# The order of the k-tiles inside a unit of matmuls, and the start of two moving operands

## The chip, the cores and the metric
The kernel runs on one core of one Trainium2 chip. The metric is the device time of one execution in microseconds (us).

## The reference
One decoder layer over 256 prompt tokens with 16 learned meta tokens ahead of them, and 8 sample tokens. It computes, with RMS norms ahead of both halves and at the end:

```python
h = rmsnorm(x, norm1_g)
z = h @ w_in                       # u, cg, bg, q, k, v, o, gates, g_a, g_b
conv_out, sc = causal_dwconv(cg * u, sc0, w_shortconv)
a_out = bg * conv_out
hb, (c, n, m) = mlstm_sequence(qh, kh, vh, ig, lf, state0, first)
mix = sigmoid(g_a) * a_out + sigmoid(g_b) * (sigmoid(o) * hb)
x = x + mix @ w_out
up, fc = causal_dwconv(rmsnorm(x, norm2_g) @ w_up, fc0, w_ffconv)
x = x + (silu(up[..., D_FF:]) * up[..., :D_FF]) @ w_down
```
D_MODEL is 2048, D_FF is 5632, there are 8 heads, all values are fp32. The outputs are the final norm of x and the new states.

## The kernel before
Features lie on the partitions and tokens in the columns. A product with fp32 accuracy is made from three products in the type fp32r: each operand is split into a high part and the rest, and hi x hi, hi weights x low data and low weights x hi data are summed in one PSUM bank.

All large products go through one routine. A **unit** (`unit`, line 1517) is 8 k-tiles of 128 rows of a weight matrix (6 in the last unit of a down strip), times 128 output columns. It makes three runs over its k-tiles: w_hi x data_hi (line 1526), w_hi x data_lo (line 1530), w_lo x data_hi (line 1534); each step is one weight load of 128 x 128 and one matmul. A **strip** (`strip`, line 1539) is two units, that is 16 k-tiles (three units and 22 k-tiles in `down_strip`, line 1666), accumulated in one bank. Four banks and four weight slots go round.

The order of the strips is written out. For each of 8 heads, `front` and `back` on the tensor engine run 16 strips on xh/xl (`mix_strip`, line 1556): strip 0 makes the head's queries (268 columns, starting at column C0 = 12), strip 1 the keys and strips 2 and 3 the values (280 columns); strips 4 to 9 make u, C, B and the three gates of the first 128 features of the head, strips 10 to 15 those of the other 128 (268 columns). After strip 4 come small matmuls and transposes for the scores (line 1587 and `turn`, line 1405), after strip 10 those for the head's values and state. Then 16 strips of the output projection on mh/ml (`out_strip`, `out_unit`, 266 columns), then twice (c = 0, 1) 44 strips of the up-projection on x2h/x2l (`up_strip`, 266 columns) and 16 strips of the down-projection on hh/hl (`down_strip`, 264 columns).

One row of k-tile data on a partition takes 280 x 4 = 1120 bytes in xh and xl, MW x 4 = 272 x 4 = 1088 bytes in x2h, x2l, mh and ml, and 264 x 4 = 1056 bytes in hh and hl. A weight k-tile takes 512 bytes. The layout puts xh at byte 34,432 of a partition (a multiple of 64), x2h at 34,464 (xh's place and 32 bytes), mh at 134,432 and the weight slots at multiples of 512 and 128 bytes. With MX = 4 (line 48) the data of x2 and of mix start 16 bytes into their rows.

Other engines: SP loads the raw weights of a unit once its slot is free; ScalarE makes w_hi (line 713) after the unit that used the slot has ended (`unit_used`); VectorE makes w_lo (line 984), takes finished banks out of PSUM (`evacuated`), writes mh/ml (lines 1245, 1248), x2h/x2l (lines 1280, 1283) and hh/hl (lines 1339, 1341), and GpSimd takes part in the gates and in the product of the feed-forward part. `unit` waits once for w_hi and once for w_lo; in its first run it takes waits tied to a k-tile: `evacuated` at k-tile 2 of a strip's last unit (so that the next strip's bank is free), and `tiles_ready` where the data are fresh.

## Time and profile before

| | us |
|---|---|
| median of 2 runs | 1700.74 (1700.73 to 1700.75) |
| the profiled execution | 1700.78 |
| its span | 1699.0 |
| PE matmul busy / weight load busy | 1688.1 / 1682.0 |
| VectorE, ScalarE, GpSimd busy | 1194.5, 766.9, 479.8 |
| chain that ended last: PE | 99% |

PE's matmuls overlap each other in the records (one lasts some 285 ns while the next starts 122 ns later), so its pace is read from the starts: a row of the view in order of time gives the start of a run of eight, and eight matmuls later the next row's start. The granted clock is 1.00 in all stretches but the first microseconds and the end. The DMA engines are busy 78% of the time in the first half and 62% in the second.

### The profile page before, as it was taken

What the parts mean: (1) busy time and instruction counts of PE and PEld (TensorE: products, weight loads), DVE (VectorE), ACT (ScalarE), POOL (GpSimd) and SP (SyncE); (2) the same over time, 40 slices, a digit from 0 to 9 for tenths busy, and PEclk for the clock granted to TensorE, in tenths of its full rate; (3) what the DMA queues carried; (4) which work ended last, traced back from release to release, by engine and by line L of the source; (5) the groups of instructions that cost most, each with busy time, mean ns of one, the idle gap of its engine ahead of it and who ended that gap; (6) DMA issues with size and microseconds to landing.
All of it is one profiled execution on the core that took longest, in us unless ns stands there. A gap on an engine that the chain in (4) does not pass through costs nothing.

```text
span 1699.0 us, 37193 instructions
## 1 busy us (share of the span) xinstructions
PE 1688.1 (99%) x13726; PEld 1682.0 (99%) x13726; DVE 1194.5 (70%) x1901; ACT 766.9 (45%) x916; POOL 479.8 (28%) x501
## 2 busy tenths in 40 slices
PE   9999999999999999999999999999999999999997
PEld 8999999999999999999999999999999999999997
DVE  5875857677585767758688877877455777777554
ACT  6545435353443535344444554544333434334443
POOL 4432414242241524224333222221000222222220
PEclk9999999999999999999999999999999999999999
DMA  8788786878778687787766666656666666666663
GB/s 204 192 222 199 197 212 168 216 177 219 192 190 216 166 216 179 212 194 195 193 177 186 189 175 184 185 173 176 183 181 182 182 179 179 179 179 178 183 176 120
DMA packets 591165, 318.80 MB, mean 188 GB/s; under 512 B 17684, under 2 KB 585988, under 8 KB 588988
## 3 DMA queue, kind: packets, MB, share of 16 engines
q1 hardware_dynamic: 578564, 292.99, 63.8%
q10 hardware_dynamic: 10448, 21.57, 5.0%
q0 software_dynamic: 2064, 2.92, 0.8%
q8 instruction: 72, 1.18, 0.3%
q14 instruction: 17, 0.14, 0.0%
HBM read 305.09 MB, written 12.78 MB: 187 GB/s over the span
## 4 chain that ended last, share of the span: by engine, by line
PE 99%; ACT 0%; POOL 0%; DVE 0%; issue 0%; ACTq 0%; POOLq 0%; DVEq 0%
PE strip L1526 32%; PE strip L1530 32%; PE strip L1534 32%; PE aux L1405 1%; PE aux L1413 1%; PE strip L1457 0%; PE aux L1587 0%; PE aux L1477 0%; PE strip L1470 0%; PE aux L1617 0%; PE aux L1616 0%; PE aux L1630 0%; PE strip L1405 0%; PE aux L1621 0%; PE aux L1622 0%; PE aux L1614 0%
## 5 line engine op out<-in xcount | busy, mean ns | idle before, releaser
L713 ACT ACTIVATE w_hi<-w_raw 128x1024 fp32r<-128x1024 f32 x557 | 588.6, 1060 | 787.7 <-PE strip L1534 755.9
L984 DVE TENSOR_TENSOR w_lo<-w_raw,w_hi 128x1024 fp32r<-128x1024 f32 x556 | 708.7, 1278 | 296.5 <-ACT w_hi L713 295.8
L1526 PE MATMUL strip<-xh,w_hi 128*128 128x268 f32 (+1 forms) x2016 | 290.9, 286 | 0.0
L1530 PE MATMUL strip<-xl,w_hi 128*128 128x268 f32 (+1 forms) x2016 | 290.0, 286 | 0.0
L1534 PE MATMUL strip<-xh,w_lo 128*128 128x268 f32 (+1 forms) x2016 | 290.0, 286 | 0.0
L1526 PEld LDWEIGHTS strip<-xh,w_hi 128*128 128x128 f32 x2016 | 265.1, 188 | 0.2
L1534 PEld LDWEIGHTS strip<-xh,w_lo 128*128 128x128 f32 x2016 | 265.2, 188 | 0.0
L1530 PEld LDWEIGHTS strip<-xl,w_hi 128*128 128x128 f32 x2016 | 265.2, 188 | 0.0
L1526 PE MATMUL strip<-x2h,w_hi 128*128 128x266 f32 x1408 | 200.1, 284 | 0.0
L1530 PE MATMUL strip<-x2l,w_hi 128*128 128x266 f32 x1408 | 199.9, 284 | 0.0
L1534 PE MATMUL strip<-x2h,w_lo 128*128 128x266 f32 x1408 | 199.9, 284 | 0.0
L1526 PEld LDWEIGHTS strip<-x2h,w_hi 128*128 128x128 f32 x1408 | 183.2, 189 | 0.1
L1534 PEld LDWEIGHTS strip<-x2h,w_lo 128*128 128x128 f32 x1408 | 183.2, 189 | 0.0
L1530 PEld LDWEIGHTS strip<-x2l,w_hi 128*128 128x128 f32 x1408 | 183.1, 189 | 0.0
L684 POOL TENSOR_TENSOR gg<-sg,cz 128x264 f32<-128x264 f32 x44 | 57.9, 1317 | 409.2 <-ACT sg L929 409.2
L687 POOL TENSOR_TENSOR hid<-gg,cz 128x264 f32<-128x264 f32 x44 | 73.6, 1674 | 101.7 <-DVE cz L1333 101.7
L1526 PE MATMUL strip<-hh,w_hi 128*128 128x264 f32 x704 | 102.2, 286 | 0.0
L1534 PE MATMUL strip<-hh,w_lo 128*128 128x264 f32 x704 | 101.3, 285 | 0.0
L1530 PE MATMUL strip<-hl,w_hi 128*128 128x264 f32 x704 | 101.2, 284 | 0.0
L1534 PEld LDWEIGHTS strip<-hh,w_lo 128*128 128x128 f32 x704 | 92.2, 189 | 0.0
L1530 PEld LDWEIGHTS strip<-hl,w_hi 128*128 128x128 f32 x704 | 91.9, 188 | 0.0
L1526 PEld LDWEIGHTS strip<-hh,w_hi 128*128 128x128 f32 x704 | 91.7, 188 | 0.0
(330 smaller groups left out, 1534.4 us busy)
## 6 DMA issues: line engine op xcount, KB each, us to landing
w_raw<-in_w_in SPq DMA_DIRECT2D x256, 512.0 KB, 4.5
w_raw<-in_w_up SPq DMA_DIRECT2D x176, 512.0 KB, 4.1
w_raw<-in_w_down SPq DMA_DIRECT2D x64, 512.0 KB, 4.0
w_raw<-in_w_out SPq DMA_DIRECT2D x32, 512.0 KB, 4.5
w_raw<-in_w_down SPq DMA_DIRECT2D x32, 384.0 KB, 3.4
out<-c_st ACTq DMA_DIRECT2D x8, 1024.0 KB, 7.0
c_st<-in_state_mlstm_C ACTq DMA_DIRECT2D x7, 1024.0 KB, 10.4
rb<-scratch_rows ACTq DMA_DIRECT2D x8, 270.0 KB, 5.3
```

The source lines that it names most:

```text
L684: g.tensor_tensor(gg[:, :], sg[:, :], cz[:, 0, :], ALU.mult).then_inc(gg_done, 1)
L687: g.tensor_tensor(hid[:, :], gg[:, :], cz[:, 1, :], ALU.mult).then_inc(hid_done, 1)
L713: act.activation(w_hi[:, slot, :], w_raw[:, slot, :], ACT.Copy).then_inc(hi_done, 1)
L984: v.tensor_tensor(w_lo[:, slot, :], w_raw[:, slot, :], w_hi[:, slot, :].bitcast(f32), ALU.subtract).then_inc(lo_done, 1)
L1405: return pe.transpose(out, in_, ident[0:k, 0:k])
L1413: pe.matmul(aux[1][:, 0:NM], ones[:, :], acc[:, :], start=True, stop=True)
L1526: pe.matmul(bank[b][:, 0:c1 - c0], w_hi[:, slot, w], rh[:, k0 + k, c0:c1], start=(first and k == 0), stop=False)
L1530: pe.matmul(bank[b][:, 0:c1 - c0], w_hi[:, slot, w], rl[:, k0 + k, c0:c1], start=False, stop=False)
L1534: mm = pe.matmul(bank[b][:, 0:c1 - c0], w_lo[:, slot, w], rh[:, k0 + k, c0:c1], start=False, stop=(last and k == kk - 1))
```

## The change
The change gives `unit` an argument `order`. It is the order in which each of the three runs goes through the unit's k-tiles. `range` is the order of before. `by_threes` takes 0, 3, 6, 1, 4, 7, 2, 5 (0, 3, 1, 4, 2, 5 in a unit of six). `backwards` takes 7 down to 0. The strips 1 to 9 of each head go by threes, strips 0 and 10 to 15 backwards, the up-projection of c = 1 backwards, the down-projection of c = 0 by threes; the output projection, the up-projection of c = 0 and the down-projection of c = 1 keep their order. In head 0 strips 0 and 1 are made by another routine and are not touched. The waits tied to a k-tile stay tied to that k-tile, wherever it comes. And x2h and x2l start 32 bytes earlier, the data of mh and ml start at column 0 (MM) of their rows in place of 4.

```diff
--- before.py
+++ after.py
@@ -45,7 +45,7 @@
     NM = NT - M0
     PM = TP - M0
     NF = NT - NMETA
-    MX = 4
+    MX, MM = 4, 0
     MW = (MX + NM + 7) // 8 * 8
     T2 = TP - 2 * P
     TL = NT - 2 * P
@@ -114,8 +114,8 @@
         sb("x_parts", [P, 2 * KT * NT])
         xh = nc.alloc_sbuf_tensor_at("xh", [P, KT, NT], f32r, offset=x_parts)
         xl = nc.alloc_sbuf_tensor_at("xl", [P, KT, NT], f32r, offset=x_parts + KT * NT * 4)
-        x2h = nc.alloc_sbuf_tensor_at("x2h", [P, KT, MW], f32r, offset=x_parts + 32)
-        x2l = nc.alloc_sbuf_tensor_at("x2l", [P, KT, MW], f32r, offset=x_parts + 32 + KT * NT * 4)
+        x2h = nc.alloc_sbuf_tensor_at("x2h", [P, KT, MW], f32r, offset=x_parts)
+        x2l = nc.alloc_sbuf_tensor_at("x2l", [P, KT, MW], f32r, offset=x_parts + KT * NT * 4)
         w_raw = sb("w_raw", [P, RING, KU * P])
         w_hi = sb("w_hi", [P, RING, KU * P], f32r)
         w_lo = sb("w_lo", [P, RING, KU * P], f32r)
@@ -1242,11 +1242,11 @@
                                             1.0, None, ALU.mult).then_inc(conv_step, 1)
                         if (k == 26 and jj == 0) or (k == 19 and jj == 1):
                             v.wait_ge(mixed, j + 1)
-                            v.tensor_scalar(mh[:, bass.ds(j, 1), MX:MX + NM].rearrange("p a t -> p (a t)"), mx[:, :], 1.0, None,
+                            v.tensor_scalar(mh[:, bass.ds(j, 1), MM:MM + NM].rearrange("p a t -> p (a t)"), mx[:, :], 1.0, None,
                                             ALU.mult).then_inc(mix_split, 1)
                             v.wait_ge(mix_split, j * 2 + 1)
-                            v.tensor_tensor(ml[:, bass.ds(j, 1), MX:MX + NM].rearrange("p a t -> p (a t)"), mx[:, :],
-                                            mh[:, bass.ds(j, 1), MX:MX + NM].rearrange("p a t -> p (a t)").bitcast(f32),
+                            v.tensor_tensor(ml[:, bass.ds(j, 1), MM:MM + NM].rearrange("p a t -> p (a t)"), mx[:, :],
+                                            mh[:, bass.ds(j, 1), MM:MM + NM].rearrange("p a t -> p (a t)").bitcast(f32),
                                             ALU.subtract).then_inc(mix_split, 1)
 
             front(0, first=True)
@@ -1514,29 +1514,36 @@
                 turn(aux[2][:, t * P:(t + 1) * P], sc_rows[:, t, :], P)
             turn(aux[2][:, 2 * P:2 * P + NS * H], n_rows[:, :], NS * H).then_inc(f_turned, 1)
 
-            def unit(u, slot, b, k0, kk, rh, rl, c0, c1, first, last, waits=(), frees=1):
-
-
+            def by_threes(kk):
+                return list(range(0, kk, 3)) + list(range(1, kk, 3)) + list(range(2, kk, 3))
+
+            def backwards(kk):
+                return list(range(kk - 1, -1, -1))
+
+            def unit(u, slot, b, k0, kk, rh, rl, c0, c1, first, last, waits=(), frees=1, order=range):
+
+
+                ks = order(kk)
                 pe.wait_ge(hi_done, u + 1)
-                for k in range(kk):
+                for k in ks:
                     for at_k, sm, value in waits:
                         if at_k == k:
                             pe.wait_ge(sm, value)
                     w = slice(k * P, (k + 1) * P)
                     pe.matmul(bank[b][:, 0:c1 - c0], w_hi[:, slot, w], rh[:, k0 + k, c0:c1],
-                              start=(first and k == 0), stop=False)
-                for k in range(kk):
+                              start=(first and k == ks[0]), stop=False)
+                for k in ks:
                     w = slice(k * P, (k + 1) * P)
                     pe.matmul(bank[b][:, 0:c1 - c0], w_hi[:, slot, w], rl[:, k0 + k, c0:c1], start=False, stop=False)
                 pe.wait_ge(lo_done, u + 1 + RING)
-                for k in range(kk):
+                for k in ks:
                     w = slice(k * P, (k + 1) * P)
                     mm = pe.matmul(bank[b][:, 0:c1 - c0], w_lo[:, slot, w], rh[:, k0 + k, c0:c1],
-                                   start=False, stop=(last and k == kk - 1))
+                                   start=False, stop=(last and k == ks[-1]))
                 if frees:
                     mm.then_inc(unit_used, frees)
 
-            def strip(s, u, i, b, rh, rl, c0, c1, need=(), between=None):
+            def strip(s, u, i, b, rh, rl, c0, c1, need=(), between=None, order=range):
 
 
 
@@ -1546,7 +1553,8 @@
                     waits = [(k - h * KU, sm, x) for k, sm, x in need if k // KU == h]
                     if h == 1:
                         waits.append((2, evacuated, s + 2))
-                    unit(u + h, (i + h) % RING, b, h * KU, KU, rh, rl, c0, c1, h == 0, h == 1, waits)
+                    unit(u + h, (i + h) % RING, b, h * KU, KU, rh, rl, c0, c1, h == 0, h == 1, waits,
+                         order=order)
 
             def tiles_ready(done, per, start, n):
 
@@ -1554,7 +1562,8 @@
                         (n - 2, done, start + per * (n - 1)), (n - 1, done, start + per * n)]
 
             def mix_strip(n, s, c0, c1, between=None):
-                strip(n * 16 + s, n * HEAD_U + 2 * s, 2 * s, s % RING, xh, xl, c0, c1, (), between)
+                order = by_threes if s % 16 < 10 and s > 0 else backwards
+                strip(n * 16 + s, n * HEAD_U + 2 * s, 2 * s, s % RING, xh, xl, c0, c1, (), between, order)
 
             def spread_r():
                 pe.wait_ge(diag_done, 3)
@@ -1645,10 +1654,10 @@
             back(H - 1)
 
             def out_strip(i, q, need=()):
-                strip(i * 4 + (S_B + q), i * 8 + (U_B + 2 * q), 2 * q, q, mh, ml, MX, MX + NM, need)
+                strip(i * 4 + (S_B + q), i * 8 + (U_B + 2 * q), 2 * q, q, mh, ml, MM, MM + NM, need)
 
             def out_unit(q, h, waits, frees):
-                unit(U_B + 2 * q + h, 2 * q + h, q, h * KU, KU, mh, ml, MX, MX + NM, h == 0, h == 1, waits, frees)
+                unit(U_B + 2 * q + h, 2 * q + h, q, h * KU, KU, mh, ml, MM, MM + NM, h == 0, h == 1, waits, frees)
 
             out_unit(0, 0, ((0, mix_split, KT),), 1)
             out_unit(1, 0, ((0, evacuated, S_B + 2),), 0)
@@ -1661,7 +1670,8 @@
                     out_strip(i, q)
 
             def up_strip(c, i, q, need=(), between=None):
-                strip(i * 4 + (S_C + c * S_CH + q), i * 8 + (U_C + c * U_CH + 2 * q), 2 * q, q, x2h, x2l, MX, MX + NM, need, between)
+                strip(i * 4 + (S_C + c * S_CH + q), i * 8 + (U_C + c * U_CH + 2 * q), 2 * q, q, x2h, x2l, MX, MX + NM, need, between,
+                      backwards if c == 1 else range)
 
             def down_strip(c, i, q, need=(), bank_free=None):
 
@@ -1670,7 +1680,8 @@
                     waits = [(x - k, sm, value) for x, sm, value in need if k <= x < k + kk]
                     if h == 2 and bank_free is not None:
                         waits.append((2,) + bank_free)
-                    unit(u + h, (3 * q + h) % RING, q, k, kk, hh, hl, 0, NF, h == 0, h == len(DOWN_UNITS) - 1, waits)
+                    unit(u + h, (3 * q + h) % RING, q, k, kk, hh, hl, 0, NF, h == 0, h == len(DOWN_UNITS) - 1, waits,
+                         order=by_threes if c == 0 else range)
 
             for c in range(CH):
                 if c == 0:
```

## Rows read from the trace of the kernel before

**Rows 1.** The page: busy time of each engine, share of the span and instructions.
```profile
PE 1688.1 (99%) x13726; PEld 1682.0 (99%) x13726; DVE 1194.5 (70%) x1901; ACT 766.9 (45%) x916; POOL 479.8 (28%) x501
```

**Rows 2.** Who waited: PE alone (two rows are all), then the longest of all engines.
```profile
PE aux L1413 <- POOL b_row L483: 2.1, 1, 2.1
PE aux L1729 <- DVE rfs L1015: 1.1, 1, 1.1
...
ACT w_hi L713 <- PE strip L1534: 755.9, 438, 4.9
```

**Rows 3.** Groups of PE instructions by shape: xcount | busy us, mean ns | idle.
```profile
L1526 PE MATMUL strip<-xh,w_hi 128*128 128x268 f32 x1648 | 235.9, 285 | 0.0
...
L1526 PE MATMUL strip<-x2h,w_hi 128*128 128x266 f32 x1408 | 200.1, 284 | 0.0
...
L1526 PE MATMUL strip<-hh,w_hi 128*128 128x264 f32 x704 | 102.2, 286 | 0.0
...
L1526 PE MATMUL strip<-xh,w_hi 128*128 128x280 f32 x368 | 55.1, 292 | 0.0
...
L1526 PE MATMUL strip<-mh,w_hi 128*128 128x266 f32 x256 | 36.3, 284 | 0.0
```

**Rows 4.** PE in order of time, projection of head 2, 268 columns: start, us, what.
```profile
306.85 1.14 PE L1534 MATMUL strip<-xh,w_lo 128*128 128x268 f32 x8
...
311.73 1.14 PE L1530 MATMUL strip<-xl,w_hi 128*128 128x268 f32 x8
```

**Rows 5.** The same view in head 0, strips 6 and 7.
```profile
65.29 1.15 PE L1530 MATMUL strip<-xl,w_hi 128*128 128x268 f32 x8
...
71.25 1.15 PE L1530 MATMUL strip<-xl,w_hi 128*128 128x268 f32 x8
```

**Rows 6.** The same view, head 3: strip 4's end, then small matmuls, then strip 5.
```profile
351.83 1.15 PE L1534 MATMUL strip<-xh,w_lo 128*128 128x268 f32 x8
352.82 0.84 PE L1587 MATMUL aux<-q_t,k_t 128*128 128x258 f32 x4
...
354.02 0.27 PE L1405 MATMUL aux<-ident,k_t 128*128 128x128 f32 x1
354.12 0.38 PE L1405 MATMUL aux<-ident,v_t 128*128 128x128 f32 x2
354.34 0.27 PE L1405 MATMUL aux<-ident,k_t 128*128 128x128 f32 x1
354.45 0.27 PE L1405 MATMUL aux<-ident,tails 128*128 128x128 f32 x1
```

**Rows 7.** The same view, head 3, strips of 280 columns.
```profile
335.55 1.19 PE L1530 MATMUL strip<-xl,w_hi 128*128 128x280 f32 x8
...
340.70 1.20 PE L1526 MATMUL strip<-xh,w_hi 128*128 128x280 f32 x8
```

**Rows 8.** The same view in the output projection (mh, ml).
```profile
860.08 1.14 PE L1534 MATMUL strip<-mh,w_lo 128*128 128x266 f32 x8
...
864.95 1.14 PE L1530 MATMUL strip<-ml,w_hi 128*128 128x266 f32 x8
```

**Rows 9.** The same view in the up-projection (x2h, x2l).
```profile
999.73 1.14 PE L1530 MATMUL strip<-x2l,w_hi 128*128 128x266 f32 x8
...
1004.60 1.14 PE L1526 MATMUL strip<-x2h,w_hi 128*128 128x266 f32 x8
```

**Rows 10.** The same view in the first down-projection, one whole strip of 22 k-tiles.
```profile
1200.91 0.89 PE L1526 MATMUL strip<-hh,w_hi 128*128 128x264 f32 x6
...
1208.93 0.28 PE L1526 MATMUL strip<-hh,w_hi 128*128 128x264 f32 x1
```

**Rows 11.** Two stretches of 268 columns, heads 0 and 3: PE busy (x), PEclk, DMA share, GB/s.
```profile
96.16:125.41 29.25, 29.25 (x242) 1.00 0.92 248
...
355.60:389.60 34.00, 34.00 (x280) 1.00 0.59 150
```

**Rows 12.** All engines in order of time where the first down-projection starts.
```profile
1171.04 1.14 PE L1526 MATMUL strip<-hh,w_hi 128*128 128x264 f32 x8
...
1176.00 0.43 DVE L1341 TENSOR_TENSOR hl<-hid,hh 128x264 f32 x1
...
1176.88 0.89 PE L1526 MATMUL strip<-hh,w_hi 128*128 128x264 f32 x6
```

## The prediction
> **What bounds the kernel.** I read the busy times first: the tensor engine (PE) is busy 99% of the span, VectorE 70%, ScalarE 45% [rows 1]. Then who waited: PE waited twice, 2.1 us at the start and 1.1 us at the end, and the longest wait of all is ScalarE's for PE [rows 2]. So weights, evacuations and data are always there when PE comes for them, and the time is the number of matmuls times the pace of one. The counts by shape stand in [rows 3], for one of the three runs of a unit. Times three they are 4944 strip matmuls of 268 columns and 1104 of 280 on xh/xl, 4224 of 266 on x2h/x2l, 2112 of 264 on hh/hl, 768 of 266 on mh/ml: 13,152 of PE's 13,726.
>
> The pace comes from starts in order of time:
> - 268 columns: 4.88 us for 40 matmuls, **122.0 ns** [rows 4]; in another stretch 5.96 us for 48, **124.2 ns** [rows 5]
> - 280 columns: 5.15 us for 40, **128.8 ns** [rows 7]
> - 266 columns: 4.87 us for 40, **121.8 ns**, in the output projection [rows 8] and the up-projection [rows 9]
> - 264 columns: 8.02 us for the 66 of a strip, **121.5 ns** [rows 10].
>
> The granted clock is 1.00, the 2.4 GHz level, so the columns alone take 111.7, 116.7, 110.8 and 110.0 ns. Each matmul costs some **10 to 12.5 ns on top**. This extra is all that the change can act on. It isn't the weight load alone: 128-column transposes follow each other in 108 ns (0.43 us for four, [rows 6]), a pace at which their weight loads fit. It doesn't follow the other engines either: with the DMA engines at 0.92 and at 0.59 the pace is 29.25 us / 240 = 121.9 and 34.00 / 278 = 122.3 ns (two of each count only overlap the edges) [rows 11].
>
> Two things show what the extra hangs on. (1) **One shape has two paces.** Strips 6 to 10 of head 0 run at 124.2 ns, the same code on the same addresses at 122.0 elsewhere; strip 4, after the 280-column strips, is slow too, (352.82 - 351.83) / 8 = 123.8 ns, and strip 5, after the small matmuls, is fast [rows 4 to 6, 11]. So the extra depends on how a stream fell into step, and keeps till something breaks it. (2) **The place of the data.** Extra over column time is 11.5/110.0 = 10.5% at 264 columns and 12.1/116.7 = 10.4% at 280; both have rows that start at 0 or 32 bytes modulo 64. It is 11.0/110.8 = 9.9% where all rows start at 48 (x2 and mix), and 10.3/111.7 = 9.2% for the fast 268 columns, whose rows start at 48 and 16 in turn.
>
> **The change part by part.** It adds and removes no instruction, DMA or wait.
>
> *Order in the mixing strips.* 126 strips x 48 = 6048 matmuls. A row is 1120 bytes, 96 modulo 256, so before each step moves the start by 96; by threes it moves by 32 (3 x 1120 = 3360), backwards by 96 the other way. The trace has a step of 32 in the down-projection (10.5%) and of 96 in the 280-column strips (10.4%), at the same alignment: no difference, so I take nothing for the step itself. What I do take is the slow pace: it is a locking of this sequence of addresses, and another sequence will hardly lock in the same places. Slow are 5 strips of head 0 and strip 4 of eight heads, 13 x 48 = 624 matmuls x 2.1 ns = **-1.3 us**. Bounds: all remaining 5424 matmuls slow, +2.1 ns x 5424 = +11.4 us; or a pace below the fast one by as much as the slow one is above, -2.1 x 6048 = -12.7 us. No row shows a lock faster than the fast one, so I stay in the middle.
>
> *Order in up, c = 1, and down, c = 0.* Half of 4224 and half of 2112, 3168 matmuls. The step of x2 goes from +64 to -64, that of hh from 32 to 96. By the same comparison **0**, bounds -2.1 x 3168 = -6.7 and +6.7 us.
>
> *x2 rows from 48 to 16 modulo 64.* If the 268-column rows average their two starts, 9.2% = (9.9% + f) / 2, then f = 8.5%: 110.8 x 1.085 = 120.2 ns in place of 121.8; as the strides differ between those rows and the lengths too, I take three quarters, -1.2 ns x 4224 = **-5.1 us**. Bounds: 0, and the whole -1.6 x 4224 = -6.8 us; on the other side +0.5% of 110.8, the worst class seen, 0.6 x 4224 = +2.5 us.
> A rule speaks against this gain. The Trainium skill, SBUF — State Buffer, in the note on cachelines of the section on the DMA port swizzle, says that reads pay for each crossing into a new 16-byte line. All these starts are multiples of 16, the number of lines is the same before and after, and by that rule this term is 0 and the sum smaller by 5.1 us. The trace doesn't decide it: it has no two starts for one shape except through (2).
>
> *mix rows from 48 to 32 modulo 64.* They enter the 10.4% class: +0.6 ns x 768 = **+0.4 us**; bounds -1 and +1.
>
> *Waits.* The wait for `evacuated` tied to k-tile 2 comes as 6th or 7th matmul in place of 3rd, 0.4 to 0.5 us later. It never held PE, so cost 0; later is only safer, and the next strip still comes behind it. In the first down strip k-tile 11 now comes second in its unit, not fourth; it needs the tiles up to the 20th, and only the last, 22nd, is made late, at 1176.43 us against 1176.88 for the unit that reads it [rows 12]. There it stays the last of its run, some 0.6 us after that start; about 1 us of slack is left. VectorE's writes to mh and x2 have the same sizes; 70% busy, they hide any few ns. Nothing moves on SP's or GpSimd's queue: their loads wait for slots that come free at the same count of matmuls. A PE faster by 1% asks DMA for 1% more, from 0.92 at most. **0.**
>
> *Sum:* 1700.8 of the profiled execution (span 1699.0 and 1.8 around it, 0.04 above the median of 1700.74) - 1.3 - 5.1 + 0.4 = 1694.8; taken from the median, **1694.7 us**.
>
> **Rivals.**
> (B) *The new orders lock at a better pace.* For it: one sequence already has two paces, so a third is near. Against: four strides (32, 64, 96, and 96 at 280 columns) all have 9.2 to 10.5%. At half the mirrored step, -1.05 ns x 9216 = -9.7, with the sum 1685; the whole would be 1675.
> (C) *Nothing changes:* order and start do not matter, the two paces come from the small matmuls ahead. Then 1700.7, or 1699.4 if only the slow strips go. The Trainium skill, TensorE: Matmul & The Clock Gate, in the steps of what happens when a matmul is issued, gives the engine two independent read ports, so that loading the next weights takes nothing from the moving data; by it the order could not matter. The extra of 10 ns in the trace is more than that page's fixed 2.5 ns per matmul, which speaks against its being the whole story.
> (D) *The mixing strips lock at the slow pace,* after the start of head 0 or after each head's small matmuls, and keep it: +11.4 without the 1.3 that would be saved, so 1700.7 + 11.4 - 4.7 = 1707.4; with the 3168 others slow too +6.7, 1714. It decides if more than 4.7 / 0.0021 = 2240 matmuls, some 47 of 126 strips, are slow beyond the 13 of now. For it: head 0 stayed slow for five strips once it was; nothing in between restores the fast pace. Against: most heads fall into the fast one.
>
> **How the numbers follow.** Forecast (1690 to 1699) 0.42, B 0.22, C 0.16, D 0.20. The range leaves out the deep end of B and the far end of D: **1682 to 1708**. The likeliest case's own range is 1690 to 1699. A difference under 2%, 34 us, is what a measurement of this kernel can hardly tell from none; it would take 3.7 ns from each of 9216 matmuls, a third of the extra (0.03), or add as much (0.01). Within 2%: 0.96.
>
> **What would show it.** In the trace after, starts of runs of eight: 268 and 280 columns at 122.0 and 128.8 ns in all strips, strips 4 and head 0's 6 to 10 no longer at 124; up-projection c = 0, whose order stays, at 120.6 ns against 121.8 shows the place alone, c = 1 the same; output projection 122.4; down c = 0 and c = 1 equal. PE still waits only twice. Wrong if c = 0 of up keeps 121.8 (place has no price), if c = 0 and c = 1 of up or of down differ (order has one), or if the mixing strips show a pace of their own.

## The result, and the profile after

The changed kernel takes **1714.5 us** (1714.22 to 1714.78), the kernel before 1700.74: ratio 1.0081 [1.0064, 1.0097]. The forecast was 1694.7, with a range up to 1708. The profiled execution took 1714.22 us with a span of 1712.5, 13.5 us more than the span before.

The page's busy times of the changed kernel, then its waits on PE (line, releaser, us in all, times, longest):

```profile
PE 1701.6 (99%) x13726; PEld 1695.5 (99%) x13726; DVE 1194.0 (70%) x1901; ACT 767.7 (45%) x916; POOL 478.0 (28%) x501
```
```profile
PE aux L1413 <- POOL a L484: 2.1, 1, 2.1
PE aux L1740 <- DVE rfs L1015: 1.1, 1, 1.1
```

All 13.5 us are PE's own [rows 1]; the two waits have the length they had [rows 2]. So no wait was added: the matmuls follow each other more slowly. PE in order of time (start, us, what), changed kernel. Head 2, 268 columns backwards (7 x 8 matmuls between the two starts); head 3, 280 columns by threes (56); head 3, 268 columns by threes (96):

```profile
320.48 1.15 PE L1541 MATMUL strip<-xh,w_lo 128*128 128x268 f32 x8
...
327.36 1.15 PE L1533 MATMUL strip<-xh,w_hi 128*128 128x268 f32 x8
...
337.58 1.21 PE L1537 MATMUL strip<-xl,w_hi 128*128 128x280 f32 x8
...
344.86 1.21 PE L1541 MATMUL strip<-xh,w_lo 128*128 128x280 f32 x8
...
358.67 1.15 PE L1541 MATMUL strip<-xh,w_lo 128*128 128x268 f32 x8
...
370.54 1.15 PE L1541 MATMUL strip<-xh,w_lo 128*128 128x268 f32 x8
```

6.88 us / 56 = 122.9 ns, 7.28 / 56 = 130.0 and 11.87 / 96 = 123.6, where [rows 4, 7] have 122.0 and 128.8. The output projection (56 matmuls), the up-projection with c = 0 (48) and c = 1 (48), and one whole strip of the first down-projection (66):

```profile
866.36 1.14 PE L1541 MATMUL strip<-mh,w_lo 128*128 128x266 f32 x8
...
873.22 1.14 PE L1533 MATMUL strip<-mh,w_hi 128*128 128x266 f32 x8
...
1005.57 1.15 PE L1541 MATMUL strip<-x2h,w_lo 128*128 128x266 f32 x8
...
1011.49 1.15 PE L1541 MATMUL strip<-x2h,w_lo 128*128 128x266 f32 x8
...
1213.20 1.13 PE L1533 MATMUL strip<-hh,w_hi 128*128 128x264 f32 x8
...
1221.20 1.01 PE L1533 MATMUL strip<-hh,w_hi 128*128 128x264 f32 x7
...
1420.70 1.15 PE L1541 MATMUL strip<-x2h,w_lo 128*128 128x266 f32 x8
...
1426.62 1.15 PE L1541 MATMUL strip<-x2h,w_lo 128*128 128x266 f32 x8
```

That is 122.5 ns [rows 8: 121.8], 5.92 / 48 = 123.3 for both halves of up [rows 9: 121.8], and 8.00 / 66 = 121.2 for down [rows 10: 121.5]. The next table has the mean distance in ns from one start to the next over a whole stage (between two strips too, but not across other work on PE), with the total against before. The last three columns are kernels of the experiments: in the first only the rows are moved, in the second only the orders are changed, in the third only the weights are moved.

```
stage (matmuls)          before  after   us      rows only  orders only  weights moved
strips 1-3, 280 (1104)   128.74  129.89  +1.26   128.74     129.88       128.75
strip 4 (384)            124.00  123.66  -0.13   124.00     123.66       123.71
strips 5-10 (2304)       122.30  123.50  +2.76   122.30     123.50       122.34
strips 11-15, 0 (2256)   122.06  122.93  +1.96   122.06     122.93       123.61
output (768)             121.67  122.51  +0.65   122.53     121.69       123.34
up c=0 (2112)            121.67  123.33  +3.51   123.34     121.67       123.33
down c=0 (1056)          121.42  121.22  -0.21   121.40     121.20       122.42
up c=1 (2112)            121.67  123.33  +3.52   123.34     123.33       123.34
down c=1 (1056)          121.56  121.53  -0.03   121.54     121.54       122.61
sum                                      +13.3
```

13.3 of 13.5 us are in this table: 5.9 in the mixing strips, 7.0 in up, 0.65 in the output projection. The two paces of before are gone in the mixing strips of 268 columns: none stands at 122.1 and none at 124.2; the new orders run at 123.6 and 122.9 in all eight heads.

### The profile page after: what moved, and what is told of

It is laid out like the page before. It is cut to its first block, busy times and chain, and to the rows that moved or that the text cites. A ratio compares the mean times of both kernels' runs of the same rounds, so it can differ in the third digit from the quotient of the medians.

```text
span 1712.5 us, 37193 instructions
## 1 busy us (share of the span) xinstructions
PE 1701.6 (99%) x13726; PEld 1695.5 (99%) x13726; DVE 1194.0 (70%) x1901; ACT 767.7 (45%) x916; POOL 478.0 (28%) x501
## 4 chain that ended last, share of the span: by engine, by line
PE 99%; ACT 0%; POOL 0%; DVE 0%; issue 0%; ACTq 0%; POOLq 0%; DVEq 0%
PE strip L1533 32%; PE strip L1541 32%; PE strip L1537 32%; PE aux L1405 1%; PE aux L1413 1%; PE strip L1457 0%; PE aux L1596 0%; PE aux L1477 0%; PE strip L1470 0%; PE aux L1626 0%; PE aux L1625 0%; PE aux L1639 0%; PE strip L1405 0%; PE aux L1622 0%; PE aux L1630 0%; PE aux L1631 0%
```

## Experiments

### The two halves of the change

Rows only: `MX = 4` stays for x2, whose tensors start 32 bytes earlier, and `MM = 0` for mix.
```diff
+    MX, MM = 4, 0
-        x2h = nc.alloc_sbuf_tensor_at("x2h", ..., offset=x_parts + 32)
+        x2h = nc.alloc_sbuf_tensor_at("x2h", ..., offset=x_parts)
```


> Kernel before with the moved rows alone: x2h/x2l 32 bytes earlier, mix data at column 0, all orders as before. Theory 1 (place and order each have their own price, and the prices add): the up-projection runs at 123.2 ns per matmul in both halves (as c = 0 did in the changed kernel, whose order stayed), so +1.5 ns x 4224 = +6.3 us, the output projection at 122.4 ns, +0.7 x 768 = +0.6 us; together 1707.6 us. Theory 2 (only the order counts; c = 0 of the up-projection got slower because it fell into another step after the mixing strips): the up-projection stays at 121.7 ns and the time at 1700.7.

Orders only: the change's `unit`, `strip`, `mix_strip`, `up_strip` and `down_strip`, with `MX` for mix too and the rows left where they were.


> The changed kernel with the rows of x2 and mix where they were before; the orders as changed. Theory 1 (place and order add): mixing strips +6.0 us as in the changed kernel, output projection and up-projection c = 0 back at 121.7 ns, up-projection c = 1 backwards at 122.1 ns (its 123.4 less the 1.5 ns of the place), +0.8 us, down c = 0 -0.2 us: 1707.3 us. Theory 2 (order alone): all of the loss stays, 1714.5. Theory 3 (place alone): 1700.7.

Rows only took 1708.2 us, ratio 1.0046 [1.0029, 1.0062]; orders only 1710.0, ratio 1.0055 [1.0038, 1.0071]. Up-projection c = 0, rows only (48 matmuls), then orders only (56; in its c = 0 nothing is changed):

```profile
1000.01 1.15 PE L1526 MATMUL strip<-x2h,w_hi 128*128 128x266 f32 x8
...
1005.93 1.15 PE L1526 MATMUL strip<-x2h,w_hi 128*128 128x266 f32 x8
```
```profile
999.81 1.14 PE L1537 MATMUL strip<-x2l,w_hi 128*128 128x266 f32 x8
...
1006.62 1.14 PE L1541 MATMUL strip<-x2h,w_lo 128*128 128x266 f32 x8
...
1410.52 1.15 PE L1541 MATMUL strip<-x2h,w_lo 128*128 128x266 f32 x8
...
1416.44 1.15 PE L1541 MATMUL strip<-x2h,w_lo 128*128 128x266 f32 x8
```

123.3 against 121.6 ns, over the whole stage 123.34 against 121.67: the rows alone cost up 1.7 ns. At 1410 us the backwards order alone costs c = 1 as much, 123.3. Both causes work, each where its code is. They don't add: 7.7 and 9.5 us are more than the 14.0 that the changed kernel, with both, takes over the same 1700.5. The difference is up c = 1. From its first start to that of down c = 1 it takes 3.5 us more with the rows moved, 3.5 with the order turned and 3.5 with both, each time at 123.3 ns. In the changed kernel the backwards order there cost nothing on top of the moved rows.

### Is it the place, or the distance from the weights?

The weights 32 bytes further on, all data left alone; and data and weights 32 bytes further on together.
```diff
-        w_hi = sb("w_hi", [P, RING, KU * P], f32r)
+        w_at = (nc.sbuf_base + 31) // 32 * 32
+        sb("w_parts", [P, 2 * RING * KU * P + 16])
+        w_hi = nc.alloc_sbuf_tensor_at("w_hi", ..., offset=w_at + 32)
```


> Kernel before with w_hi and w_lo 32 bytes later; data and orders as before. The distance from weights to x2 is then the one of the changed kernel (data 32 bytes nearer). Theory A (the extra time per matmul comes from the matmul's data read and the next weight load meeting in memory, so it hangs on the distance of the two modulo some width): up-projection at 123.2 ns, +6.3 us, and mixing and down strips change too, by up to 2 ns either way. Theory B (only the data's own place counts): nothing changes, 1700.7 us.

```diff
-        x_parts = (nc.sbuf_base + 31) // 32 * 32
-        sb("x_parts", [P, 2 * KT * NT])
+        x_parts = (nc.sbuf_base + 31) // 32 * 32 + 32
+        sb("x_parts", [P, 2 * KT * NT + 8])
-        base = (nc.sbuf_base + 223) // 512 * 512 + 288
+        base = (nc.sbuf_base + 223) // 512 * 512 + 320
```


> Kernel before with everything 32 bytes later: xh/xl, x2h/x2l, mh/ml, hh/hl, w_raw, w_hi, w_lo. Every distance from data to weights is the one of before, every place is another. Theory A (distance): all stages at the pace of before, up-projection and output projection 121.7 ns, 1700.5 us. Theory B (the place of the data itself): output projection and up-projection change (the up-projection's rows now start at 16 modulo 64, as in the changed kernel: 123.2 ns, +6.3 us), 1707 us.

Weights moved: 1714.5 us, ratio 1.0081 [1.0064, 1.0097], with not one order or data row changed. All moved: 1700.5, ratio 0.9998 [0.9988, 1.0007]. Up c = 0 with the weights moved (48 matmuls), then with all moved (48):

```profile
1003.41 1.15 PE L1536 MATMUL strip<-x2h,w_lo 128*128 128x266 f32 x8
...
1009.33 1.15 PE L1536 MATMUL strip<-x2h,w_lo 128*128 128x266 f32 x8
```
```profile
998.55 1.14 PE L1526 MATMUL strip<-x2h,w_hi 128*128 128x266 f32 x8
...
1004.39 1.14 PE L1526 MATMUL strip<-x2h,w_hi 128*128 128x266 f32 x8
```

123.3 ns as when the data moved, and 121.7 as before. With all moved, every stage of the table is within 0.02 ns of before. So in this one shift of 32 bytes the address had no price by itself; the **distance between the data row and the weights** has one. This is why averages over "the start modulo 64" could not hold.

That both the changed kernel and this one take 1714.5 us is chance: here it is 7.0 us in up, 2.2 in down, 1.3 in the output projection, 3.5 in mixing. And the 3.5 in mixing are no new pace. Strips 6 to 10 and 11 to 15 still run at 122.1 or at 124.2 ns, but others of them are slow: head 0 is at 122.1 from strip 5 on, and strips 11 to 15 are at 124.2 from head 2 on. Head 3, strip 12 (40 matmuls):

```profile
399.12 1.16 PE L1528 MATMUL strip<-xh,w_hi 128*128 128x268 f32 x8
...
404.09 1.16 PE L1536 MATMUL strip<-xh,w_lo 128*128 128x268 f32 x8
```

4.97 / 40 = 124.2 ns, where before has 122.1. For the 268-column strips the 32 bytes changed which of the two paces a strip takes, not the paces. (`ident` and what else lies behind the weights moved along, so the small matmuls may have had a part in which one; the up-projection has none in between.)

### What each order costs

One order for each head, in one kernel. Heads 6 and 7 compute something else: head 6 reads the data of k-tile 0 for every k, head 7 the weights of k-tile 0.
```diff
+            orders = (range, threes, backwards, fives, evens_then_odds, pairs_four_apart)
+                how = dict(order=orders[n]) if n < 6 else dict(data=lambda k: 0) if n == 6 else dict(weights=lambda k: 0)
```


> Kernel before with another order in the mixing strips of each head. Head 0 as before, 1 by threes, 2 backwards, 3 by fives (0 5 2 7 4 1 6 3), 4 evens then odds, 5 in pairs four apart (0 4 1 5 2 6 3 7); in head 6 every matmul reads k-tile 0's data with its own weights, in head 7 every matmul loads k-tile 0's weights with its own data (these two compute something else). Theory O (the step from one data start to the next counts): strips 5 to 9 run at 122.0 ns in head 0's order, 123.5 by threes, 123.0 backwards, and the others between 120 and 125, each head steady; head 7 like head 0's order if only the data's steps count. Theory R (it is only the step the stream falls into after the small matmuls): the orders differ by no more than the two paces of before, 122.0 and 124.1, and show no other values. Head 6 gives the pace with no step at all.

1705.0 us. Strips 7 and 8 of heads 1 (48 matmuls), 2 (56) and 7 (56):

```profile
170.57 1.16 PE L1526 MATMUL strip<-xh,w_hi 128*128 128x268 f32 x8
...
176.50 1.16 PE L1526 MATMUL strip<-xh,w_hi 128*128 128x268 f32 x8
...
268.81 1.15 PE L1530 MATMUL strip<-xl,w_hi 128*128 128x268 f32 x8
...
275.69 1.15 PE L1534 MATMUL strip<-xh,w_lo 128*128 128x268 f32 x8
...
768.71 1.14 PE L1526 MATMUL strip<-xh,w_hi 128*128 128x268 f32 x8
...
775.55 1.14 PE L1530 MATMUL strip<-xl,w_hi 128*128 128x268 f32 x8
```

By threes 123.5, backwards 122.9, weights of one k-tile 122.1. Over the whole of strips 6 to 10: in order 124.1 (head 0, its slow pace of [rows 5]), threes 123.6, backwards 122.9, fives 123.3, evens then odds 123.3, pairs four apart 123.7 (122.5 in strips 11 to 15), one data row 122.2, one weight tile 122.1. The last is the fast pace of the untouched order. So which of the unit's weight tiles is read, all of them multiples of 512 bytes apart, does not matter, and it is through the **data rows** that the order acts. The one data row is no cure either: at 280 columns it took 133.3 ns against 128.7. The change's two orders, which cost it 5.9 us in mixing, have the same paces here as in its own trace.

### Places, widths and starts

These are other places (modulo 64), columns and orders. In the first two kernels, output and up take 260 of 266 columns from four different starts, and in the first the mixing strips start at another column in each head, with 64 or 32 weight columns in heads 6 and 7.
```diff
+                    c0 = (12, 0, 2, 4, 6, 10, 12, 12)[n]
+                ... x2h, x2l, ((4, 6, 8, 10), (5, 7, 9, 4))[c][q], (the same) + 260
```


> Kernel before with the data windows moved by whole columns (the result is another). Mixing strips of 268 columns start at column 12 in head 0, then 0, 2, 4, 6, 10 in heads 1 to 5; heads 6 and 7 start at 12 but load only 64 and 32 columns of weights per matmul. In the output projection and the up-projection c = 0 each matmul takes 260 columns, starting at column 4, 6, 8, 10 in the strips q = 0 to 3, that is at 48, 56, 0, 8 modulo 64 from the weights; c = 1 at columns 5, 7, 9, 4. Theory A (data and weight reads meet): with 64 and 32 columns of weights the extra of 10.3 ns per matmul falls to about a half and a quarter, so 117 and 115 ns; the pace depends on the place by 1 to 2 ns, and column 0 (32 bytes modulo 64 away from 8 or 40, same class as itself modulo 32) equals no 16-byte class of column 4 and 12. Theory C (the extra has nothing to do with the weight read): 122.0 ns in heads 6 and 7 too.

The second: x2 rows 32 bytes earlier and mix rows 32 further on, so both from 16 modulo 64; with mix all operands of the small matmuls lie 32 bytes further on. Another order in each head.
```diff
+                order=(range, sevens, there and back, swapped pairs, one turned, threes, in twos, range)[n]
```


> As the run before, with x2 32 bytes earlier and mix 32 bytes later, so the same columns lie at 16, 24, 32, 40 modulo 64 from the weights; with it the places of 8 bytes are complete. Mixing strips start at column 12 in all heads and take other orders: head 0 as before, 1 by sevens (0 7 6 5 4 3 2 1), 2 forward then backward (0 1 2 3 7 6 5 4), 3 swapped pairs (0 2 1 3 4 6 5 7), 4 one turned (7 0 1 2 3 4 5 6), 5 by threes, 6 in twos (0 1 4 5 2 3 6 7), 7 as before. Theory A with steps: orders made mostly of the step +1 (4, 6) stay near 122.0 to 122.5 ns, those of the step -1 (1) go with backwards, 123.0; no order is faster than 122.0. Places: 16 modulo 64 slower than 48 by some 1.5 ns as in the moved rows.

Then the starts of the x2 and mix rows, with all columns. The first two of these four also shift (`c0`) or narrow (`c1`) the mixing strips' columns by head, so that they compute other values; the last two try orders in down.
```diff
+    MX, MM = 6, 5      (then 0, 6; 6, 1; 2, 3; x2h at x_parts in the second and third)
+                    c0 = (12, 1, 3, 5, 7, 9, 11, 8)[n]                        (the first)
+                    c1 = c0 + (268, 264, 260, 256, 266, 252, 248, 240)[n]     (the second)
+                    order=backwards if c == 0 else by_threes                  (the third)
+                    order=evens_then_odds if c == 0 else backwards            (the fourth)
```


> Kernel before with other places: x2 at 56 and mix at 52 modulo 64 (48 and 48 before), 266 columns as before. Mixing strips of 268 columns start at column 12 in head 0, then 1, 3, 5, 7, 9, 11, 8 (another result). Theory A (the distance from data to weights sets the pace): x2 at 56 and mix at 52 run at another pace each, between 120 and 124 ns; columns 1 and 9 (4 modulo 32) share a pace, so do 3 and 11 (12 modulo 32), as the stride of 96 visits every multiple of 32. If only the 16-byte line counts, 52 goes with 48 and 56 too, 121.7 ns.

> As the run before, with x2 at 0 and mix at 56 modulo 64. Mixing strips start at column 12 and have 268, 264, 260, 256, 266, 252, 248, 240 columns in heads 0 to 7 (another result). Mix at 56 here must equal x2 at 56 in the run before. If the extra per matmul is a fixed cost the pace falls by 0.42 ns per column, from 122.0 to about 110.3 at 240 columns; if the weight loads set a floor, it stays above 108; if reads meet, the fall is uneven, by up to 2 ns from the line.

> Kernel before with x2 at 24 and mix at 36 modulo 64; down-projection backwards in c = 0 and by threes in c = 1. Theory A: paces of their own between 120 and 124 ns for x2 and mix; the down-projection by threes 121.2 ns as in the changed kernel, now in c = 1, backwards between 121 and 123.

> Kernel before with x2 at 40 and mix at 44 modulo 64; down-projection evens then odds in c = 0 and backwards in c = 1. Theory A: paces of their own between 120 and 124 ns for x2 and mix; backwards as in the run before. If one of the eight places tried so far is faster than 48 with 121.7 ns by 1 ns, a kernel with it gains 4 us in the up-projection.

Times: 1702.7 and 1699.3 for the first two, 1715.4, 1687.8, 1709.8 and 1708.5 for the others. The first two and the 1687.8 compute fewer columns, so these times are no gains. Paces in ns, from start to start over whole strips (6 to 10 in the mixing strips):

```
266 columns, rows in order, rows start at (modulo 64):
x2    0: 123.3   16: 123.3   24: 123.3   40: 122.8   48: 121.7   56: 122.5
mix  32: 122.5   36: 123.3   44: 123.3   48: 121.7   52: 125.0   56: 122.5
260 columns, x2, the four strips of a group from four starts:
      0: 119.9    4: 122.2    8: 122.5   16: 119.1 or 118.9   20: 123.3   24: 120.1
     28: 119.1   32: 120.1   36: 122.9   40: 121.3   48: 120.0   52: 121.9   56: 122.5   60: 118.9
268 columns from column (before: 12):
      0: 124.2    2: 125.0    4: 122.1    6: 125.0    8: 124.2   10: 125.0   12: 122.1 or 124.2
      1: 125.8    3: 122.5    5: 127.5    7: 122.5    9: 125.8   11: 122.5
      (in strips 11-15 column 1: 126.7, 5: 125.0, 9: 126.7)
more orders, 268 columns, strips 6-10: sevens 122.9, there and back 122.9, threes 123.6, in twos 123.3,
      swapped pairs 123.3 (121.7 in 11-15), one turned 122.1 (124.2 in 11-15)
down, 264 columns: range 121.4 to 121.6, threes 121.2 to 121.4, backwards 122.3 to 122.6, evens-odds 122.6
columns from 12 on: 268: 122.1   266: 122.5   264: 120.8   260: 118.3   256: 117.8   252: 117.5   248: 114.2   240: 112.1
```

For 266 columns the 48 of before is the best start in both lists. For 260 columns it is not: starts of 16 and of 60 went at about 119 ns against 120.0. One strip of each, up c = 0, from 48 in the first kernel and from 16 in the second (40 matmuls each):

```profile
942.22 1.12 PE L1526 MATMUL strip<-x2h,w_hi 128*128 128x260 f32 x8
...
947.01 1.12 PE L1534 MATMUL strip<-x2h,w_lo 128*128 128x260 f32 x8
```
```profile
940.15 1.13 PE L1526 MATMUL strip<-x2h,w_hi 128*128 128x260 f32 x8
...
944.92 1.11 PE L1534 MATMUL strip<-x2h,w_lo 128*128 128x260 f32 x8
```

That is 119.8 and 119.3 ns: the same two starts that differ by 1.7 ns one way at 266 columns differ by 0.5 to 1.1 the other way at 260. A start has no price that holds for another length.

In the mixing strips columns 0 and 8, 2 and 10, 1 and 9, 3 and 11, each pair 32 bytes apart, give the same; x2 at 16 and at 48, also 32 apart, differ by 1.7 ns. A reading that fits both, argued and not tested by itself: what counts is the set of row starts modulo 256. The 1120-byte rows of xh step by 96 and pass all eight multiples of 32, so a shift by 32 gives the same eight; the 1088-byte rows of x2h step by 64 and pass only four, and 16 and 48 are different fours. The weights-moved kernel agrees in mixing, where 122.1 and 124.2 stayed. Its down strips do not agree: their rows step by 32 modulo 256 and a unit of eight passes all eight too, yet 32 bytes took them from 121.4 to 122.4. They have a unit of six besides, so this is no clean test. Strips of 240 columns in head 7 of the second of these four (40 matmuls):

```profile
755.14 1.06 PE L1534 MATMUL strip<-xh,w_lo 128*128 128x240 f32 x8
...
759.62 1.06 PE L1530 MATMUL strip<-xl,w_hi 128*128 128x240 f32 x8
```

4.48 / 40 = 112.0 ns for 100.0 ns of columns; at 268 columns 122.0 for 111.7. The extra goes up and down between 10.0 (260 columns) and 12.5 ns (252) and is 12.1 at both 240 and 280. So it does not grow with the length, as the percentage of the columns that the prediction computed with would have it.

### Does the width of the weight tile matter?

x2 rows at 16; each matmul multiplies only the first columns of its weight tile, so most outputs are not computed: (128, 112, 96, 80, 64, 32, 16, 128) by head, 32 in output and up c = 0, 64 in up c = 1.
```diff
-                    w = slice(k * P, (k + 1) * P)
+                    w = slice(k * P, k * P + cols)
```


> Kernel before with narrower weight loads (another result): in the mixing strips 128, 112, 96, 80, 64, 32, 16, 128 columns of weights in heads 0 to 7, in the output projection 32, in the up-projection 32 (c = 0) and 64 (c = 1); x2 is moved by 32 bytes as in the changed kernel, so with full weights the output projection ran at 121.7 ns and the up-projection at 123.2 ns. Theory S (data and weight reads disturb each other only where they start): output projection 121.7, up-projection 123.2 ns still, whatever the width. Theory L (they meet all along, and the earlier 121.7 ns at 64 and 32 columns in the mixing strips was chance): the up-projection falls below 122 and the gap between the two places closes; mixing strips fall step by step with the width. Theory D (the 10 ns are the data stream's own, and the weights only shift them): all narrow ones end at one pace near 121.7.

1697.8 us. Up c = 0 with 32 weight columns (40 matmuls), and c = 1 with 64 (48):

```profile
1001.23 1.11 PE L1526 MATMUL strip<-x2h,w_hi 128*32 128x266 f32 x8
...
1005.96 1.11 PE L1534 MATMUL strip<-x2h,w_lo 128*32 128x266 f32 x8
...
1400.36 1.15 PE L1530 MATMUL strip<-x2l,w_hi 128*64 128x266 f32 x8
...
1406.28 1.15 PE L1530 MATMUL strip<-x2l,w_hi 128*64 128x266 f32 x8
```

118.3 and 123.3 ns on the same rows; with all 128 weight columns it was 123.3. In mixing 112 to 16 weight columns gave 121.7, 122.5, 123.3, 121.7, 121.7 and 120.8 (128: 122.1 or 124.2), and the 64 and 32 of the earlier kernel the same 121.7 each, far from the 117 and 115 expected there. Reading fewer weights can take 5 ns off, or nothing, with no order in it. None of the theories written ahead gives both of up's numbers, so which reads get in each other's way stays open.

### Can the good pieces be put together?

There-and-back in strips 1 to 4, swapped pairs in 11 to 15, threes in down; then the same without the swapped pairs and with strip 4 in its old order.
```diff
+                order = there_and_back if 0 < s < 5 else swapped if s > 10 else range     (first)
+                order = there_and_back if 0 < s < 4 else range                            (second)
+                    ... waits, order=by_threes)                                           (down, both)
```


> A version put together from the paces seen so far: rows where they were before; strips 1 to 4 of each head there and back (0 1 2 3 7 6 5 4: 128.0 ns at 280 columns in the earlier run against 128.8, 122.5 in strip 4 against 124.0), strips 5 to 10 and 0 in the order of before, 11 to 15 in swapped pairs (121.7 against 122.0), both down-projections by threes (121.2 to 121.4 against 121.4 to 121.6). If each stage keeps the pace it had there: -0.9 - 0.6 - 0.6 - 0.4 = -2.5 us, 1698 us. Against it: the pace depends on what the stream comes from, so a stage may fall into another one; then between 1697 and 1704.

> The kernel before with two orders alone: strips 1 to 3 of each head there and back (0 1 2 3 7 6 5 4), both down-projections by threes; rows and all other strips as before. Theory I (a stage's pace depends on what runs ahead of it): strips 1 to 3 at 128.0 ns (-0.9 us), down -0.3 us, and strips 4 and on either keep 124.0, 122.1, 122.0 (1699.2 us) or fall to 124.1 from strip 5 to 10 as in the combined version (1703 us). Theory J (each order has its own pace wherever it stands): 1699.2 us.

1706.1 us, ratio 1.0030 [1.0019, 1.0041], and 1703.4, ratio 1.0016 [1.0007, 1.0025]: both slower. In the second the pieces did what was hoped: strips 1 to 3 at 128.1, strip 4 at 122.4, down at 121.2 and 121.3, together -1.7 us. But strips 5 to 10, whose code is untouched, took the slow pace in heads 1 to 7: +4.2 us. Head 3, end of strip 4 (16 matmuls), then strips 7 and 8 (56), second kernel:

```profile
350.59 1.14 PE L1530 MATMUL strip<-xl,w_hi 128*128 128x268 f32 x8
...
352.55 0.84 PE L1597 MATMUL aux<-q_t,k_t 128*128 128x258 f32 x4
...
368.19 1.16 PE L1534 MATMUL strip<-xh,w_lo 128*128 128x268 f32 x8
...
375.14 1.16 PE L1526 MATMUL strip<-xh,w_hi 128*128 128x268 f32 x8
```

Strip 4 now ends at 1.96 / 16 = 122.5 ns [rows 6: 123.8], and the strips behind the small matmuls go at 6.95 / 56 = 124.1 [rows 11: 122.3 there]. The gain ahead of the small matmuls was lost behind them. In the first kernel the swapped pairs ran at 123.3 in all heads, behind 122.1 in head 0 and behind 124.2 in the others, in place of the 121.7 seen above. So the pace ahead of them did not decide it. Above, another order ran in strips 5 to 10 and the operands of the small matmuls lay 32 bytes elsewhere; which of the two counted is not shown. The up-projection, also untouched, kept 121.67 in both halves and both kernels.

### The entry alone

There, strip 4's pace could have been the cause, or the time at which strip 5 starts. The last experiment changes only what comes between: head n does n more transposes of 128 columns ahead of strip 5.
```diff
+                        for _ in range(n):
+                            turn(aux[3][0:rows, 0:P], tails[:, 0:rows], P)
```


> The kernel before with n more transposes of 128 columns in head n, 0 to 7, between strip 4 and strip 5; they repeat the last one there. All strips, orders and addresses are as before. 28 transposes of some 110 ns would add 3.1 us. Theory I (two paces, chosen by how the stream is entered): strips 5 to 10 run at 122.1 or at 124.2 ns by head, nothing else. Theory J (the pace is a property of shape and place): 122.0 ns in every head from 1 on.

1707.3 us. Strips 7 and 8 of head 3, then of head 4 (56 matmuls each):

```profile
368.30 1.16 PE L1526 MATMUL strip<-xh,w_hi 128*128 128x268 f32 x8
...
375.26 1.16 PE L1530 MATMUL strip<-xl,w_hi 128*128 128x268 f32 x8
...
468.67 1.14 PE L1526 MATMUL strip<-xh,w_hi 128*128 128x268 f32 x8
...
475.50 1.14 PE L1530 MATMUL strip<-xl,w_hi 128*128 128x268 f32 x8
```

124.3 and 122.0 ns. Head 0, with no more transposes, is as before; heads 1, 2, 3, 5, 6 and 7 run strips 6 to 10 at 124.2, head 4 at 122.0, and every other stage is as before. Same code, addresses and order from strip 5 on: the entry chooses between the two paces, and the choice lasts through six strips, 288 matmuls, until the small matmuls ahead of strip 11. The paces give +3.6 us; the 28 more transposes, at the 108 ns of [rows 6], +3.0; the span grew by 6.6.

The second kernel of "Places, widths and starts" says the same without one instruction more. In its head 0 order, data rows and weights are those of before. Of what PE reads there only the operands of the small matmuls lie 32 bytes further on. And strips 6 to 10 ran at 122.1 and 11 to 15 at 124.2, the reverse of before.

## Why the prediction was wrong

**What bounds the kernel**: right. PE waited twice, its count of matmuls is the same, and 13.3 of 13.5 us are in the pace of its matmuls. That the extra over the columns is all that the change can act on held too, and so did the zero for waits.

**The step that failed first: "x2 rows from 48 to 16 modulo 64", -5.1 us.** With the rows moved alone it measured +1.67 ns x 4224 = +7.0 us, outside the bound of +2.5. Of the 19.8 us between forecast and result 12.1 are in this term and 7.2 in that of the mixing strips. The inference behind it, that 268-column rows average a dear start at 48 and a cheap one at 16, mixed three things that the runs took apart: the extra is 10 to 12.5 ns for each matmul and does not grow with its columns, and the better start at 266 columns is not the better one at 260; a start has no price without the weights (32 bytes for all: ratio 0.9998); and rows of another stride took 32 bytes without a new pace. The stated bounds were percentages of other shapes. A bound from the widest difference seen for one shape, the 2.1 ns of [rows 4, 5], would have held it here: +2.1 x 4224 = +8.9.

The rule of the Trainium skill weighed there (SBUF — State Buffer, cachelines of 16 bytes) gave 0 for this term and was nearer than -5.1. The runs do not bear it out as the whole story: x2 rows from 0, 16 and 48, all multiples of 16, take 123.3, 123.3 and 121.7 ns.

**"Order in the mixing strips", 0 for the step itself and -1.3 for the slow pace.** Half right and of no use: the slow pace did go, as argued. But these two orders have paces of their own, 123.6 by threes and 122.9 backwards, and nearly all 6048 now run slower than on the fast one: +5.9 us in all, within the bounds of -12.7 to +11.4. The comparison that gave 0 set data strides of different shapes side by side, and one that sees only the stride is blind to where a row lies against the weights read at the same time.

**"Order in up, c = 1, and down, c = 0", 0.** Up: +1.67 ns x 2112 = +3.5 us when alone, nothing on top of the moved rows. So the 0 came out in the changed kernel by luck. Down: -0.2 us for 1056 matmuls.

**"mix rows from 48 to 32", +0.4**: measured +0.65 us. The mechanism behind it, a class of starts, is the same that failed for x2.

**The rivals.** D had the direction, and its far end, 1714, had the time, by luck: the mechanism was another. Its price was the old slow pace, 124.2, taken by more strips, and no strip of the changed kernel has it; the x2 term, the largest, was carried in it with the wrong sign. The slow pace did spread as D describes in the two later kernels, where the untouched strips 5 to 10 fell into it. B had asked for a better pace; among ten other orders none beat 122.1 in strips 6 to 10, though some did elsewhere: 121.7 for swapped pairs in strips 11 to 15, 128.1 there and back at 280 columns. C fell with the first halves: order and place both matter. The rule beside C (the Trainium skill, TensorE: Matmul & The Clock Gate: two independent read ports, so that loading weights takes nothing from the moving data) is not borne out: weights 32 bytes further on, with the data in place, made the distance between up-projection matmuls 1.7 ns longer.

**Shown**: the pace depends on the distance between data and weights, on the order of the data rows, and on how the stream was entered; not on the address by itself (one shift, 32 bytes), nor on which weight tile of a unit is read. **Open**: what in the chip makes it so. The widths gave no rule, and no run tells reads of weights and of data apart from what happens to the output. That no other combination beats before was not shown either; nothing tried did.

## What to carry to other kernels

When TensorE is never kept waiting and still needs some 10 ns a matmul more than its columns, order and relative place of its operands can matter: here by up to 0.9%, each time to the worse. They can't be read off averages over other shapes, not even shapes six columns shorter: try them, one for each head or stage in a single kernel, and compare starts over whole strips. A gain in one stage counts only with the stages behind it, since an untouched stage can take another pace from how it is entered; judge the whole kernel. Bound an untried address or order to both sides, by no less than the widest difference that the trace has for one shape. Even that can be too narrow: this trace had 2.1 ns, and later places cost 3.3 (mix at 52) and 5.4 (column 5).

## What the runs showed of the hardware beyond that

The extra is no jitter but a repeated pattern. Distances in ns between successive starts in one strip of the up-projection's c = 0, twelve matmuls:

```
before      125 121 123 118 | 125 121 122 119 | 125 121 122 118
rows moved  118 125 122 128 | 118 125 122 128 | 119 125 121 129
```

It comes back within 1 ns after four matmuls, in the other strips of that half as well, and four rows of 1088 bytes are 17 x 256. So a matmul's time depends on its own operands and its neighbours', and a pace is the mean over such a pattern: its lowest distance stayed at 118 and its highest went from 125 to 129. The two paces of the mixing strips are two patterns on the same addresses. But two patterns can have one pace: before, c = 1 of up goes 123 118 120 126, and both halves are at 121.67. The last distance of a strip, to the first matmul of the next, belongs to the pattern. Without it the two halves come out as 121.75 and 121.57, a difference that is not there.

Most paces lie on steps. In units of one column's time at the granted clock (1/2.4 ns), 121.67, 122.50, 123.33 and 125.00 ns for 266 columns are 292, 294, 296 and 300, and 122.08 and 124.17 for 268 are 293 and 298; 122.78 (x2 at 40) and 123.61 (by threes) lie between steps. Rows from 0, 16 and 24 and the backwards order, with unlike patterns, all end at the 296. Why these values, no run shows.

The start of the program varies by itself: in the profiled execution of the second combined kernel, the first ten warm-up matmuls (`warm`) ended 0.9 us earlier than before, with the same code. First before, then that kernel:

```profile
4.45 2.42 PE L1413 MATMUL aux<-acc,ones 128*128 128x266 f32 x5
```
```profile
4.45 1.56 PE L1413 MATMUL aux<-acc,ones 128*128 128x266 f32 x5
```

They start some 445 ns apart at first and 224 ns apart later, and in that kernel this happened at 5.2 us in place of 7.0. The granted clock is given as 1.00 there in both, so the trace does not say why. All later work kept these 0.9 us. That is why the kernel's span grew by only 1.5 us where its stages took 2.4 more, and why a single execution says little about a difference below 1 us.
